# First recurrent mixer of a fused seven-stage network: four modulation units moved to later stages, the border to the next stage in the common form, the last turns gathered behind one output unit

## The chip, the cores and the metric

The kernel runs on one core of one Trainium2 chip. The metric is the time of one execution in microseconds (us), as the device reports it. Before the change three runs gave 1424.58, 1425.66 and 1426.38 us, the median being 1425.66.

Engines in this text: TensorE (PE: products; its weight loads are PEld), VectorE (DVE), ScalarE (ACT), GpSimd (POOL) and SyncE (SP), which issues all transfers from HBM.

## The reference

The input x has 256 tokens of 1024 values. It goes through six sublayers (feed-forward, mLSTM mixer, feed-forward, feed-forward, Mamba-2 mixer, feed-forward) and one hybrid attention layer. Each sublayer has this form:

```python
def swiglu(h, w1, w3, w2):
    return (jax.nn.silu(h @ w1) * (h @ w3)) @ w2

def sublayer(x, fn, g_pre, g_post, shift, scale, gate, weight):
    hmod = rms_norm(x, g_pre) * (1 + scale[:, None, :]) + shift[:, None, :]
    y = rms_norm(fn(hmod), g_post)
    return x + weight * gate[:, None, :] * y
```

`shift`, `scale` and `gate` are the modulation: three vectors of 1024 per sublayer, from a matrix of 1024 x 9216 per layer of three sublayers:

```python
c_act = jax.nn.silu(c)
mod = (c_act @ ada_w[i] + ada_b[i]).reshape(B, N_SUB, 3, D_MODEL)
```

The mLSTM mixer projects to queries, keys, values and an output gate for 4 heads, computes the heads, normalises each, multiplies it by the sigmoid of the gate and ends with the output product `hs.astype(h.dtype) @ w_out`, with `w_out` of 1024 x 1024. All is float32.

## The kernel before, in words

**Stages.** The seven sublayers are stages n = 0 to 6 (`KIND`): ffn, ml, ffn, ffn, mb, ffn, hy. Stage 1 (ml) is the first recurrent mixer, stage 2 the second feed-forward. Each engine has one program that is written out by hand, stage after stage; its instructions run in that order, and semaphores order the engines among each other.

**Weights.** All weights come in units of 1 MB (128 x 2048 float32), numbered through the whole kernel; `FIRST[n]` is a stage's first. A unit is loaded by SyncE into one of five places of a ring (`raw`), rounded by ScalarE (`hi(u)`, L558) and its remainder is computed by VectorE (`lo(u)`, L1704, or in four quarters by `lo_part`, L1709). The remainder is written over the raw unit. TensorE computes each float32 product as three: high x high, high x low, low x high. A place is free when TensorE has used the unit for both halves of the tokens (t = 0 and 1, 128 tokens each); SyncE waits for that before the load. At the borders before stages 1, 3, 4, 5 and 6 the next stage's second unit (`outside`) and its fourth (`landing`) are loaded into two other areas, so that they can come before ring places are free. Stage 2 does not have that.

**Modulation units.** The modulation matrices come in units of 1 MB as well (`load_ada`, into two places `araw` that alternate). VectorE multiplies each with c and sums it up in two products of 128 x 1024 (`ada(v)`, L1714). They serve no product of TensorE; they only have to be done before the stage that they modulate: shift and scale before the stage's input is made (`mod_columns`), the gate before its output is added (`gate_columns`). `ADA_FIRST` and `ADA_BLOCKS` set which are done in which stage. The mixer does ten, 26 to 35: six among its recurrence, one each behind `denominator(3)`, behind `turned_lo(0, ...)` and behind `turned_lo(1, ...)`, and the tenth in the border. Stages 2 and 3 do 18 each, two ahead of block 2 and two per block in blocks 2 to 9.

**End of the mixer.** The last pair of heads is made by VectorE (`heads_out(1)`, L2030) once ScalarE has the sigmoid of the output gate (L752). TensorE turns the heads by 128 x 128 (`turn_am`, L1367), ScalarE copies them out as high parts (`turned_hi`, L790) and VectorE as remainders (`turned_lo`, L2061). The output product has four units, each used for t = 0 and t = 1 (`down`). Units 0 and 1 need the first pair of heads, units 2 and 3 the last.

**Border.** Between two stages: y (the output product) of one half of the tokens is squared by ScalarE (`square_y`, L623) and multiplied by the gate by VectorE (`gated_y`, L1801); GpSimd makes the norm (L474, L475); VectorE makes the new x (`new_x`, L1808); ScalarE squares it (L615); GpSimd makes the second norm; VectorE scales it (`normed_x`, L1770); TensorE turns it (`turn_x`, L1154); ScalarE and VectorE modulate it and split it into high part and remainder (L639, L643, L1779). TensorE hides this for t = 0 behind the output product for t = 1, and for t = 1 behind the first products of the next stage (`first_two`). `boundary(n, late)` is that border on ScalarE and VectorE: the common form has `late` False; the form behind stage 1 has `late` True and takes in the remainders of the next stage's first four weights and a modulation unit.

**Feed-forward.** 11 blocks of two up units and, two blocks behind, one down unit; each block is six groups of twelve products and four turns of 128 x 128 (L1263).

## Time and profile before

| | |
|---|---|
| median of three runs | 1425.66 us (1424.58 to 1426.38) |
| profiled execution: span from the first to the last instruction | 1421.9 us |
| profiled execution's own time around the span | not given on the page |
| mean granted TensorE clock | 0.998 of the full 2.4 GHz |
| busy: PE, PEld, DVE, ACT, POOL | 1394.5, 1185.4, 1024.9, 719.7, 90.4 us |
| moved from HBM | 339.07 MB, 238 GB/s on average |
| stage 1 with its border | about 228 to 345 us |
| stage 2, stage 3 | about 324 to 516 us, 516 to 705 us |

A line of the timeline has its start in us from the span's start, its length in us, the engine, the line of the kernel, the operation with what it writes and reads, how many instructions are merged, and in brackets how long the engine was idle before it and what released it. The ends of products are modelled, since products are pipelined: where one follows at once, the distance of two starts tells the time of one. "L1045" is the helper through which all weight products go, "L1704" is that of all whole remainders, "L558" that of all roundings.

### The profile page before, as it was taken

How to read it: one execution, taken by the hardware profiler on the slowest of the kernel's cores; microseconds unless marked ns; L12 is line 12 of the kernel's file. 1: busy time of each engine (PE TensorE's matmuls, PEld its weight loads, DVE VectorE, ACT ScalarE, POOL GpSimd, SP SyncE). 2: the span in 40 equal slices, each digit the busy share in tenths (PEclk: the TensorE clock that was granted, in tenths of full speed). 3: DMA queues.
4: the chain of work that ended last, by engine and by line, in shares of the span. 5: the costliest groups of instructions: out<-in, count | busy, mean ns of one | idle time of the engine just before them, and what ended most of it. 6: DMA issues, size and time to landing. Idle time of an engine off the chain costs nothing.

```text
span 1421.9 us, 18024 instructions
## 1 busy us (share of the span) xinstructions
PE 1394.5 (98%) x7310; PEld 1185.4 (83%) x7310; DVE 1024.9 (72%) x1296; ACT 719.7 (51%) x931; POOL 90.4 (6%) x118
## 2 busy tenths in 40 slices
PE   9999999998999999999999999999999999999997
PEld 8788888977888878888789978788888889998886
DVE  5887677987987668777767976678745654664865
ACT  5543356456444455343565676554334644555433
POOL 1000001001000010000000352100000100000000
PEclk9999999999999999999999999999999999999999
DMA  9898865855988848888535522478755454445542
GB/s 385 339 351 303 319 247 198 320 193 201 391 308 298 325 162 324 318 311 332 200 135 186 209 74 89 178 299 336 283 206 207 178 204 167 148 170 186 199 149 111
DMA packets 50498, 339.07 MB, mean 238 GB/s; under 512 B 6720, under 2 KB 8432, under 8 KB 10352
## 3 DMA queue, kind: packets, MB, share of 16 engines
q1 hardware_dynamic: 50416, 337.92, 63.8%
q8 instruction: 58, 0.95, 0.3%
q14 instruction: 24, 0.20, 0.0%
HBM read 336.81 MB, written 2.66 MB: 239 GB/s over the span
## 4 chain that ended last, share of the span: by engine, by line
PE 78%; DVE 12%; ACT 4%; DMA 2%; issue 2%; POOL 1%; SPq 0%; ACTq 0%; DVEq 0%; POOLq 0%
PE ps L1045 76%; DVE wlo L1704 4%; DMA raw<-units 2%; DVE hf L2126 2%; DVE M L1714 1%; ACT whi L558 1%; PE ps L1263 1%; PE ps L1154 1%; ACT hf L639 0%; POOL base L474 0%; POOL ssx L475 0%; DVE xboth L1779 0%; DVE wlo L1709 0%; PE ps L1528 0%; DVE xboth L2061 0%
## 5 line engine op out<-in xcount | busy, mean ns | idle before, releaser
L1045 PE MATMUL ps<-whi,xboth 128*128 128x512 f32 x2864 | 912.2, 393 | 6.5 <-DVE wlo L1709 1.7
L1045 PEld LDWEIGHTS ps<-whi,xboth 128*128 128x128 f32 x2864 | 538.3, 188 | 125.4 <-issue 4.7
L1704 DVE TENSOR_TENSOR wlo<-raw,whi 128x2048 fp32r<-128x2048 f32 x212 | 486.2, 2298 | 178.5 <-ACT whi L558 178.0
L1045 PE MATMUL ps<-wlo,xboth 128*128 128x512 f32 x1432 | 558.5, 390 | 0.0
L558 ACT ACTIVATE whi<-raw 128x2048 fp32r<-128x2048 f32 x218 | 416.9, 1915 | 170.8 <-DMA raw<-units 170.7
L1045 PEld LDWEIGHTS ps<-wlo,xboth 128*128 128x128 f32 x1432 | 269.5, 188 | 52.6
L1045 PE MATMUL ps<-xboth,whi 128*128 128x256 f32 (+1 forms) x1152 | 254.6, 310 | 0.1
L1045 PEld LDWEIGHTS ps<-xboth,whi 128*128 128x128 f32 x1152 | 187.9, 190 | 12.4 <-ACT hf L829 0.3
L1045 PE MATMUL ps<-xboth,wlo 128*128 128x256 f32 x704 | 198.1, 281 | 0.0
L1714 DVE SCALAR_TENSOR_TENSOR M<-M 128x1024 f32<-128x1024 f32 x160 | 189.3, 1220 | 0.1
L1045 PEld LDWEIGHTS ps<-xboth,wlo 128*128 128x128 f32 x704 | 133.9, 190 | 0.0
L722 ACT ACTIVATE xboth<-ps 128x512 fp32r<-128x512 f32 x44 | 26.3, 598 | 129.1 <-PE ps L1263 129.1
L718 ACT ACTIVATE M<-ps 128x256 f32<-128x256 f32 x88 | 33.2, 380 | 91.0 <-PE ps L1045 88.5
L474 POOL TENSOR_SCALAR base<-ssx 128x1 f32<-128x1 f32 x28 | 17.6, 629 | 950.5 <-ACT M L623 615.1
L1913 DVE TENSOR_TENSOR M<-M,ps 128x256 f32<-128x256 f32 x88 | 36.0, 417 | 29.4 <-ACT M L718 29.2
L1919 DVE TENSOR_TENSOR xboth<-ps,xboth 128x512 fp32r<-128x512 f32 x44 | 30.3, 689 | 21.8 <-ACT xboth L722 21.7
L2126 DVE SCALAR_TENSOR_TENSOR hf<-hf,cols 128x253 f32<-128x253 f32 (+2 forms) x72 | 36.8, 553 | 7.8 <-ACT hf L829 6.8
L1779 DVE TENSOR_TENSOR xboth<-hf,xboth 128x256 fp32r<-128x256 f32 x42 | 17.9, 446 | 25.0 <-ACT xboth L643 24.6
L639 ACT ACTIVATE hf<-ps,shT,g1T 128x128 f32<-128x128 f32 x60 | 23.8, 446 | 20.5 <-PE ps L1154 20.5
L615 ACT ACTIVATE M<-x 128x512 f32<-128x512 f32 x28 | 17.7, 631 | 26.7 <-DVE x L1808 24.9
L1045 PE MATMUL ps<-unit_at,xboth 128*128 128x512 f32 x120 | 28.9, 389 | 0.0
L1263 PEld LDWEIGHTS ps<-ident,M 128*128 128x128 f32 x176 | 21.7, 140 | 6.8 <-DVE M L1913 0.7
(242 smaller groups left out, 881.2 us busy)
## 6 DMA issues: line engine op xcount, KB each, us to landing
raw<-units SPq DMA_DIRECT2D x218, 1024.0 KB, 4.9
M<-ada_units SPq DMA_DIRECT2D x82, 1024.0 KB, 7.1
M<-units SPq DMA_DIRECT2D x10, 1024.0 KB, 5.3
gp<-gate_rows SPq DMA_DIRECT2D x7, 512.0 KB, 6.1
bias_copies<-bias_by_distance SPq DMA_DIRECT2D x1, 1536.0 KB, 9.6
M<-cvec SPq DMA_DIRECT2D x2, 512.0 KB, 4.4
x<-x_in SPq DMA_DIRECT2D x1, 1024.0 KB, 6.0
ada_a<-ada_units SPq DMA_DIRECT2D x1, 1024.0 KB, 20.0
```

What stands on the lines that cost most here:

```text
L558: act.activation(rounded(u), landed(u), ACT.Copy).then_inc(w_hi, 1)
L639: r = act.activation(hf[:, k, t_], ps[:, 2 * t + q // 2, (k % 4) * P:(k % 4 + 1) * P], ACT.Identity, scale=g1T[:, n, k:k + 1], bias=shT[:, ...
L718: act.activation(sil[:, t, :], ps[:, bank, 0:FB], ACT.Silu).then_inc(sil_ok[t], 1)
L722: act.activation(xhi[:, 8 + 2 * (i % 4):10 + 2 * (i % 4), :], ps[:, 6, :], ACT.Copy)\
L1045: return pe.matmul(out, lhsT, rhs, start=start, stop=stop, skip_group_check=True)
L1263: r = pe.transpose(ps[:, 6, kk * SEQ + t * P:kk * SEQ + (t + 1) * P], g[i % 2][:, t, kk * P:(kk + 1) * P], ident[:, :])
L1704: dve.tensor_tensor(rest(u), landed(u), rounded(u).bitcast(F32), ALU.subtract).then_inc(w_lo, 1)
L1714: return dve.scalar_tensor_tensor(out=w, in0=w, scalar=1.0, in1=cb, op0=ALU.mult, op1=ALU.mult, accum_out=sums[:, column:column + 1])
L1779: dve.tensor_tensor(xlo[:, k2, t_], hf[:, k2, t_], xhi[:, k2, t_].bitcast(F32), ALU.subtract)\
L1913: dve.tensor_tensor(g[i % 2][:, t, :], sil[:, t, :], ps[:, bank, FB:2 * FB], ALU.mult)\
L1919: dve.tensor_tensor(xlo[:, j:j + 2, :], ps[:, 6, :].rearrange("p (a b) -> p a b", b=SEQ), xhi[:, j:j + 2, :].bitcast(F32), ALU.subtract).t ...
L2126: r = dve.scalar_tensor_tensor(out=cacc[:, q, sh:SEQ], in0=cin[:, q, 0:SEQ - sh], scalar=cols[:, col:col + 1], in1=cacc[:, q, sh:SEQ], op0 ...
```

## The change

It does these things:

- Mixer, stage 1: six modulation units (26 to 31) instead of ten. Those behind `denominator(3)`, behind both `turned_lo` and in the border are gone; `ada_done` and `mod_columns` for the next stage stand ahead of `heads_out(1)`.
- Stages 2 and 3 do 20 each, 32 to 51 and 52 to 71: blocks 4 and 6 have three. The gate's columns of stage 2 are made in its block 4.
- Stage 2's second and fourth weight units are loaded outside the ring, as those of the other stages, and the border is the common form, without its `late` branches.
- VectorE: `heads_out(1)` stands ahead of the remainder of the third output unit.
- TensorE: the output product goes (t, unit) = (0,0), (1,0), (0,1), (0,2), (0,3), (1,1), (1,2), (1,3) instead of (0,0), (0,1), (0,2), (0,3), (1,0), ... (1,3). The turns of the last pair stand together behind (0,0) instead of half inside and half behind (0,1).

```diff
-ADA_FIRST = {0: 8, 1: 26, 2: 36, 3: 54, 5: 72}
-ADA_BLOCKS = {0: 9, 2: 9, 3: 9, 5: 6}
+ADA_FIRST = {0: 8, 1: 26, 2: 32, 3: 52, 5: 72}
+ADA_LAST = {0: 25, 1: 31, 2: 51, 3: 71, 5: 83}
+def ada_in_block(n, i):
+    if i > {0: 9, 2: 9, 3: 9, 5: 6}[n]:
+        return 0
+    return 3 if n in (2, 3) and i in (4, 6) else 2
...
-        outside = {FIRST[n] + 1: n for n in (1, 3, 4, 5, 6)}
-        landing = {FIRST[n] + 3: n for n in (1, 3, 4, 5, 6)}
+        outside = {FIRST[n] + 1: n for n in range(1, 7)}
+        landing = {FIRST[n] + 3: n for n in range(1, 7)}
...
-                        sp.wait_ge(a_used[u in outside], (ADA_FIRST[n - 1] + 2 * ADA_BLOCKS[n - 1] - 2 - EARLY) // 2 + 1)
+                        sp.wait_ge(a_used[u in outside], (ADA_LAST[n - 1] - EARLY) // 2 + 1)
...
-                    if n == 3:
+                    if n in (2, 3):
                         sp.wait_ge(w_lo, u0 + 4)
                     load_ada(v)
                     load(down_unit(n, 0))
-                    if n in (3, 5):
+                    if n in (2, 3, 5):
                         sp.wait_ge(w_used, u0 + 2)
                     load_ada(v + 1)
...
-                        for _ in range({6: 1, 7: 1, 8: 0, 9: 0, 10: 2, 15: 2}.get(u, u > 10)):
+                        for _ in range({6: 1, 7: 1, 10: 2, 11: 1, 12: 1}.get(u, 0)):
                             load_ada(v)
...
+                    load(FIRST[n + 1] + 1)
...
# ScalarE, stage 1
-                    hi(u0 + 16)
-                    boundary(n, True)
+                    for u in range(16, 19):
+                        hi(u0 + u)
+                    boundary(n)
...
# TensorE, stage 1
-                    for t in range(T):
-                        for u in range(4):
-                            if t == 0 and u == 2:
-                                turn_am(1, (1,))
-                            pe.wait_ge(S["ml_lo"], 2 * (u // 2) + t + 1)
-                            middle = None
-                            if (t, u) == (0, 1):
-                                middle = lambda: turn_am(1, (0,))
-                            if (t, u) == (1, 3):
-                                middle = lambda: turn_x(n + 1, 0)
-                            r = down(u0 + 12 + u, 2 * u, t, start=(u == 0), stop=(u == 3), middle=middle)
...
+                    for t, u in ((0, 0), (1, 0), (0, 1), (0, 2), (0, 3), (1, 1), (1, 2), (1, 3)):
+                        if (t, u) == (1, 0):
+                            turn_am(1, (0, 1))
+                        pe.wait_ge(S["ml_lo"], 2 * (u // 2) + t + 1)
+                        r = down(u0 + 12 + u, 2 * u, t, start=(u == 0), stop=(u == 3),
+                                 middle=(lambda: turn_x(n + 1, 0)) if (t, u) == (1, 3) else None)
...
# VectorE, border: the late branches are gone
-                if late:
-                    ada(ADA_FIRST[n] + 9)
-                    ada_done(ADA_FIRST[n] + 9)
-                    mod_columns(n + 1)
-                else:
-                    lo_part(u + 2, 1)
-                    lo_part(u + 2, 2)
+                lo_part(u + 2, 1)
+                lo_part(u + 2, 2)
...
# VectorE, feed-forwards
-                            ada(v + 1)
-                            v += 2
-                        if n == 0 and i == 4:
+                        for k in range(1, some):
+                            ada(v + k)
+                        v += some
+                        if n in (0, 2) and i == 4:
                             ada_done(v - 1)
-                            gate_columns(0)
+                            gate_columns(n)
...
# VectorE, stage 1
-                    ada(v + 6)
                     after_piece(5, u0 + 8)
                     turned_lo(0, (0, 1))
-                    ada(v + 7)
+                    ada_done(v + 5)
+                    mod_columns(n + 1)
+                    heads_out(1)
                     after_piece(7, u0 + 8)
-                    heads_out(1)
                     turned_lo(1, (0,))
                     lo(u0 + 15)
                     turned_lo(1, (1,))
-                    ada(v + 8)
-                    boundary(n, True)
+                    lo(u0 + 16)
+                    boundary(n)
```

How this moves instructions, in the order in which they stand. VectorE, end of the mixer, before, from ahead of the last pair of heads to the new x of the first half. The wide products on `M,sums` are modulation units, `wlo` are remainders of weights, `M<-ps 128x256 x4` the last pair of heads, `xboth<-ps,cols,xboth` their turned remainders, `M<-ps,gp` the gated y:

```order
L1714 SCALAR_TENSOR_TENSOR M,sums<-M 128x1024 x2
L1704 TENSOR_TENSOR wlo<-raw,whi 128x2048
L2025 TENSOR_TENSOR M<-M 128x4
L2030 SCALAR_TENSOR_TENSOR M<-ps,M 128x256 x4
L2061 SCALAR_TENSOR_TENSOR xboth<-ps,cols,xboth 128x128 x4
L1704 TENSOR_TENSOR wlo<-raw,whi 128x2048
L2061 SCALAR_TENSOR_TENSOR xboth<-ps,cols,xboth 128x128 x4
L1714 SCALAR_TENSOR_TENSOR M,sums<-M 128x1024 x2
L1801 TENSOR_TENSOR M<-ps,gp 128x512 x2
L1808 SCALAR_TENSOR_TENSOR x<-M,ssx,x 128x512 x2
L1714 SCALAR_TENSOR_TENSOR M,sums<-M 128x1024 x2
L1731 TENSOR_TENSOR shT<-sums,cols 128x8
```

The same place after the change:

```order
L1732 SCALAR_TENSOR_TENSOR g1T<-modc,cols 128x8
L2008 TENSOR_TENSOR M<-M 128x4
L2013 SCALAR_TENSOR_TENSOR M<-ps,M 128x256 x4
L1703 TENSOR_TENSOR wlo<-raw,whi 128x2048
L2044 SCALAR_TENSOR_TENSOR xboth<-ps,cols,xboth 128x128 x4
L1703 TENSOR_TENSOR wlo<-raw,whi 128x2048
L2044 SCALAR_TENSOR_TENSOR xboth<-ps,cols,xboth 128x128 x4
L1703 TENSOR_TENSOR wlo<-raw,whi 128x2048
L1703 TENSOR_TENSOR unit_at_51<-M,unit_at_49 128x2048
L1708 TENSOR_TENSOR wlo<-raw,whi 128x512
L1800 TENSOR_TENSOR M<-ps,gp 128x512 x2
L1807 SCALAR_TENSOR_TENSOR x<-M,ssx,x 128x512 x2
```

Four lines of modulation units are gone (the one at the top here, two further down, and one above the rows shown), the heads stand ahead of the third output unit's remainder, and three remainders of the next stage (`wlo`, `unit_at_51`, and a quarter) stand ahead of the gated y.

TensorE, output product of the mixer, before, around the turns of the last pair (`ident,M`), which stand in two groups of four with half a block between them:

```order
L1045 MATMUL ps<-wlo,xboth 128x512
L1045 MATMUL ps<-whi,xboth 128x512
L1367 MATMUL ps<-ident,M 128x128 x4
L1045 MATMUL ps<-whi,xboth 128x512
L1045 MATMUL ps<-wlo,xboth 128x512
L1045 MATMUL ps<-whi,xboth 128x512 x2
L1045 MATMUL ps<-wlo,xboth 128x512
L1045 MATMUL ps<-whi,xboth 128x512
L1367 MATMUL ps<-ident,M 128x128 x4
L1045 MATMUL ps<-whi,xboth 128x512
```

After, the eight turns stand together behind the first block, with whole blocks on either side:

```order
L1049 MATMUL ps<-whi,xboth 128x512 x2
L1049 MATMUL ps<-wlo,xboth 128x512
L1049 MATMUL ps<-whi,xboth 128x512
L1371 MATMUL ps<-ident,M 128x128 x8
L1049 MATMUL ps<-whi,xboth 128x512
L1049 MATMUL ps<-wlo,xboth 128x512
L1049 MATMUL ps<-whi,xboth 128x512 x2
L1049 MATMUL ps<-wlo,xboth 128x512
L1049 MATMUL ps<-whi,xboth 128x512 x2
```

Each group of `whi`, `wlo`, `whi` is one high x high, high x low, low x high product of 128 x 128 by 128 x 512; a block has twelve.

VectorE, feed-forward of stage 2, around its block 4, before:

```order
L1704 TENSOR_TENSOR wlo<-raw,whi 128x2048
L1714 SCALAR_TENSOR_TENSOR M,sums<-M 128x1024 x2
L1704 TENSOR_TENSOR wlo<-raw,whi 128x2048
L1714 SCALAR_TENSOR_TENSOR M,sums<-M 128x1024 x2
L1919 TENSOR_TENSOR xboth<-ps,xboth 128x512
L1704 TENSOR_TENSOR wlo<-raw,whi 128x2048
L1913 TENSOR_TENSOR M<-M,ps 128x256 x2
```

And after:

```order
L1703 TENSOR_TENSOR wlo<-raw,whi 128x2048
L1713 SCALAR_TENSOR_TENSOR M,sums<-M 128x1024 x4
L1742 TENSOR_TENSOR gpc<-sums,cols 128x8
L1743 SCALAR_TENSOR_TENSOR gpc<-gpc,cols 128x8
L1703 TENSOR_TENSOR wlo<-raw,whi 128x2048
L1713 SCALAR_TENSOR_TENSOR M,sums<-M 128x1024 x2
L1902 TENSOR_TENSOR xboth<-ps,xboth 128x512
L1703 TENSOR_TENSOR wlo<-raw,whi 128x2048
```

The modulation unit at the block's end has become two (x4 products instead of x2), and the gate's columns of stage 2 stand behind them. Block 6, and blocks 4 and 6 of stage 3, have the x4 as well, without the gate's columns.

## Rows read from the trace of the kernel before

**Rows 1.** The page, section 1: busy time, share of the span, instructions.

```profile
PE 1394.5 (98%) x7310; PEld 1185.4 (83%) x7310; DVE 1024.9 (72%) x1296; ACT 719.7 (51%) x931; POOL 90.4 (6%) x118
```

**Rows 2.** TensorE's waits, 296 to 345: line, releaser: total, times, longest.

```profile
PE ps L1045 <- DVE wlo L1709: 1.7, 1, 1.7
PE ps L1045 <- DVE xboth L1779: 1.2, 1, 1.2
...
PE ps L1045 <- DVE wlo L1704: 0.7, 1, 0.7
```

**Rows 3.** Timeline of TensorE, turns of the last pair.

```profile
304.30 0.39 PE L1045 MATMUL ps<-whi,xboth 128*128 128x512 f32 x1
305.39 0.66 PE L1367 MATMUL ps<-ident,M 128*128 128x128 f32 x4 [0.70 <-DVE M L2030]
...
307.28 0.60 PE L1367 MATMUL ps<-ident,M 128*128 128x128 f32 x4
308.44 0.50 PE L1045 MATMUL ps<-whi,xboth 128*128 128x512 f32 x1 [0.56 <-DVE xboth L2061]
```

**Rows 4.** The chain of waits, a steady piece: start, length, what.

```profile
376.95 16.38 PE ps L1045 x72
```

**Rows 5.** Timeline of VectorE, 299 to 315.

```profile
299.77 1.22 DVE L1714 SCALAR_TENSOR_TENSOR M<-M 128x1024 f32<-128x1024 f32 x1
...
302.06 2.29 DVE L1704 TENSOR_TENSOR wlo<-raw,whi 128x2048 fp32r<-128x2048 f32 x1
...
304.46 1.66 DVE L2030 SCALAR_TENSOR_TENSOR M<-ps,M 128x256 f32<-128x256 f32 x4
...
314.21 1.41 DVE L1801 TENSOR_TENSOR M<-ps,gp 128x512 f32<-128x512 f32 x2 [0.31 <-PE ps L1045]
```

**Rows 6.** Timeline of ScalarE, 300 to 323.

```profile
300.65 0.60 ACT L752 ACTIVATE M<-ps 128x512 f32<-128x512 f32 x1 [0.31 <-PE ps L1045]
...
309.51 1.92 ACT L558 ACTIVATE whi<-raw 128x2048 fp32r<-128x2048 f32 x1 [0.46 <-DMA raw<-units]
...
322.11 1.92 ACT L558 ACTIVATE whi<-raw 128x2048 fp32r<-128x2048 f32 x1 [3.07 <-DMA raw<-units]
```

**Rows 7.** Timeline of TensorE, turns of input and of feed-forward, stage 2.

```profile
323.54 1.03 PE L1154 MATMUL ps<-ident,M 128*128 128x128 f32 x8
...
350.92 0.60 PE L1263 MATMUL ps<-ident,M 128*128 128x128 f32 x4
```

**Rows 8.** Timeline of TensorE, the same turns at three common borders.

```profile
515.91 1.09 PE L1154 MATMUL ps<-ident,M 128*128 128x128 f32 x8 [0.30 <-DVE M L1770]
...
538.99 0.60 PE L1263 MATMUL ps<-ident,M 128*128 128x128 f32 x4
...
705.00 1.09 PE L1154 MATMUL ps<-ident,M 128*128 128x128 f32 x8 [0.99 <-DVE M L1770]
...
917.30 1.09 PE L1154 MATMUL ps<-ident,M 128*128 128x128 f32 x8 [0.67 <-DVE M L1770]
```

**Rows 9.** Timeline of all engines, 697 to 699.

```profile
697.25 0.60 ACT L623 ACTIVATE M<-ps 128x512 f32<-128x512 f32 x1 [1.59 <-PE ps L1045]
...
698.37 1.28 DVE L1801 TENSOR_TENSOR M<-ps,gp 128x512 f32<-128x512 f32 x2
```

**Rows 10.** Timeline of SyncE's queue, 302 to 303.

```profile
302.54 0.43 SPq L287 DMA_DIRECT2D raw<-units  x1
```

**Rows 11.** The page, section 6: KB each, median us to landing.

```profile
raw<-units SPq DMA_DIRECT2D x218, 1024.0 KB, 4.9
```

**Rows 12.** Stretches: span, busy us of each engine, clock, DMA, GB/s.

```profile
351.00:371.00 20.00, 20.00 (x94) 16.61 (x93) 19.78 (x23) 11.12 (x10) 0.00 (x0) 1.00 1.02 424
421.50:438.30 16.80, 16.80 (x78) 13.89 (x77) 12.89 (x15) 6.62 (x6) 0.00 (x0) 1.00 0.84 310
574.00:591.00 17.00, 17.00 (x78) 14.07 (x77) 13.06 (x15) 6.90 (x6) 0.00 (x0) 1.00 0.83 310
```

**Rows 13.** Timeline of VectorE, a remainder of block 6, stage 2.

```profile
435.15 2.29 DVE L1704 TENSOR_TENSOR wlo<-raw,whi 128x2048 fp32r<-128x2048 f32 x1 [1.39 <-ACT whi L558]
```

63 lines of the change are left out of this document (23 added, 40 removed).

## Prediction, made before the result was known

> **What bounds the kernel now.** I read the page's busy line first. TensorE is busy for 1394.5 of 1421.9 us [rows 1], so the kernel ends when TensorE has got through its products, and only places where TensorE stands still can give time back. The list of TensorE's waits shows where: between 296 and 345 us, the end of the first recurrent mixer and its border to the second feed-forward, it stood idle for VectorE five times: 1.7, 1.2 and 0.7 us in the first products of the feed-forward [rows 2], behind parts of the weights and of the normalised input that VectorE still had to split, and 0.70 and 0.56 us around the turns of the mixer's last pair of heads [rows 3]. TensorE's timeline gives the losses from start to start, VectorE's and ScalarE's say what those two were doing meanwhile, and the borders of the other stages, which already have the common form, say what that form costs. All times stand against one profiled execution with a span of 1421.9 us. The page gives no time around that span; the median of the three runs, 1425.66, lies 3.8 us above it, and I carry that distance over unchanged.
>
> **The turns of the last pair.** A product takes 16.38 / 72 = 0.2275 us, a block of twelve 2.73 [rows 4]. The product at 304.30 is followed at 305.39, 1.09 us on: 0.86 lost. Four turns start at 307.28 and the product behind them at 308.44, 1.16 us on. Eight turns are busy for 1.03 us and four for 0.66 [rows 3, 7], so four cost 0.4, and 0.76 us are lost. Together 1.6 us; by idle time alone it is 0.70 + 0.56 = 1.26, the lower end. The cause is in VectorE's rows: a modulation unit from 299.77, a weight's remainder from 302.06, and only at 304.46 the four products that make the last pair's heads (L2030, 1.66 us) [rows 5]. They could have begun with ScalarE's last sigmoid out, at 300.65 + 0.60 = 301.25 [rows 6]. After the change the unit is gone and the remainder stands behind the heads, so these are made from 301.3 to 303.2 (0.2 for one small operation, then 1.66). The output phase began eighteen products before 304.53, at 300.4, so its first unit for the first half of the tokens ends at 303.2. The turns stand behind it now and find their input ready. Should the heads be late by x, TensorE waits x; I take 0, with 0.5 as upper end. Behind the turns TensorE has two blocks, 5.5 us, while ScalarE and VectorE copy the turned half out; before it had half a block. The remainder behind the heads is done at 305.4, and its unit, the third, is needed at 303.2 + 0.8 + 2 x 2.73 = 309.5.
>
> **The border.** From the turns of the new input's first half at 323.54 to the first turns of the feed-forward at 350.92 are 27.38 us [rows 7]. The same instructions between the second and the third feed-forward, where the form is the common one, take from 515.91 to 538.99, 23.08 us [rows 8]. The common form is thus worth 4.30 us here. This holds the idle times of [rows 2], 1.7 + 1.2 + 0.7 = 3.6 us, which are the lower end, and the slower starts behind them. What VectorE loses is plain: in the late form one modulation unit lies right ahead of the border and one within it, together with the remainders of all four first weights of the feed-forward. In the changed kernel the units are gone, and two weights and a quarter of the third are done ahead of y.
>
> What comes in their place is a wait ahead of the input's turns. From y's first half to these turns the chain square, norm, new x, norm, scaled x runs beside three blocks with the turns inside the last (2.5 x 2.73 = 6.8 us) in the common form, beside four in the late one. Three like borders show 0.30, 0.99 and 0.67 us of idle there [rows 8]. In the one with 0.99 VectorE began on y at 698.37, 1.1 us after ScalarE's first square of the same y at 697.25 [rows 9]. So the wait is set by how late ScalarE and VectorE come to y, whose half is done at 303.2 + 0.8 + 4 x 2.73 = 314.9 in the new order (VectorE began on it at 314.21 before [rows 5]). VectorE: from the first turned half at 305.3 it has 1.1, 2.2 (a remainder), 1.1, 2.2, 2.2 and 0.7 to do, which gives 314.8. The weight: the third unit of the feed-forward takes the place of the first output unit, which is free when both halves have been through it. That was one block after y's first half, at 316.9, and ScalarE, idle for the transfer until then, rounded what landed from 322.11 on [rows 6]: 5.2 us. Now the second half goes through that unit as the second block, so the place is free at 306.7, the unit lands at 311.9, is rounded by 313.8 and a quarter of it split by 314.6 to 315.0. Both come out just as y does. I take 0.5 us; the ends are 0 and 2.0. The upper one comes from the load issued at 302.54 and rounded from 309.51, 6.9 us [rows 6, 10], though that lay behind two modulation units; the page's median is 4.9 [rows 11].
>
> The Trainium skill would make this dearer: "DMA: Bandwidth & Descriptors", section "Bandwidth", has 6.15 us for a load of 1 MB; by it the new wait would be 0.9 us longer and the time 1421.2. The rows of this trace are shorter, and I go by them.
>
> **What moves into the feed-forwards.** The mixer has six modulation units instead of ten: VectorE is rid of 4 x 2 x 1.22 = 9.8 us [rows 5] there, SyncE of four transfers of 1 MB. The second and third feed-forward get two more each, as a third unit in blocks 4 and 6 (counted from 0), and one of them 0.4 us for the gate's columns. Two products of 1.22 us per unit make 2.4 us more for VectorE in such a block. A block takes TensorE 16.8 us, in which VectorE is busy for 12.9 [rows 12] and TensorE never idle; 3.9 us are free, 2.4 to 2.8 asked for: cost 0. The remainders also have a lead. The piece of 72 at 376.95 starts 5.9 us into block 3 [rows 4], so a block starts at 371.1, and block 7 at 438.3. The remainder made at 435.15 is of that block's last weight, used from 438.3 + 5.9 + 5.5 = 449.7 on, 12 us after it is done, and VectorE had waited 1.39 us for ScalarE before it [rows 13]. On SyncE's queue the third unit stands behind the second, and behind it the next weight's load; VectorE had read its place earlier in the same block, so SyncE need not stand. A sixth transfer makes 372 GB/s of 310. The trace has 424 GB/s at 351 to 371, with TensorE at 20.00 of 20.00 us [rows 12]. In the second feed-forward the first modulation units now wait until VectorE has split the fourth weight and TensorE has been through the second; the third feed-forward does so already and loses nothing (its 23.08 us are the measure above). Cost 0; the upper end is the third rival's price.
>
> The Trainium skill speaks against this: the same page, section "Specifications", has 358 GB/s as what HBM gives one core. By it such a block's six transfers would take 17.6 us, 0.8 more than TensorE's block, 3.0 us over the four, and the time would be 1423.3 if nothing hid it. The 424 GB/s do not bear it out for this core, so it changes no chance.
>
> **Sum.** -1.6 (turns) - 4.3 (border) + 0.5 (new wait) + 0 (feed-forwards) = -5.4 us: a span of 1416.5, a time of 1420.3. By the ends -5.9 at best (1419.8) and -1.3 + 0.5 - 3.6 + 2.0 = -2.4 at worst (1423.3), rivals aside.
>
> **Rivals.**
> - *The new border is late.* The transfer takes 6.9, or VectorE slips, since six jobs follow each other between 305 and 315 with nothing to spare. The wait is 2.0 instead of 0.5, the time 1421.8. For it: both chains end within 0.3 us of y. Against: less traffic, with no modulation unit on the way.
> - *Half of it.* The turns are covered, but the border keeps its waits at other products (the fourth weight, the input's second half), since the mixer hands VectorE over later than a feed-forward does. Only the 1.6 us are won: 1424.1. For it: VectorE has no pause from 305 on. Against: the border at 917.30 follows a mixer too and has a wait of 0.67 only [rows 8].
> - *The feed-forwards become bound by VectorE.* If in all four blocks the 2.4 us fell on the path, that is 9.6 us, the time 1429.9: slower. It decides once a block's added work passes the 3.9 us that VectorE has free and the lead of 12 us is used up. For it: VectorE is busy for 19.78 of 20.00 us at 351 to 371 [rows 12], the opening of the same feed-forward. Against: block 4 starts 17 us later, and in its like of the third feed-forward (574 to 591) VectorE is at 13.06 of 17.00.
>
> **How the numbers follow.** Forecast 0.70 (by itself 1419.3 to 1421.3), late border 0.15, half 0.10, bound feed-forwards 0.05. A measurement of this kernel can tell about 0.2%, 2.9 us, from no change, so faster means below 1422.8: 0.70 + 0.15 = 0.85; same 0.10, the half; slower 0.05. The range takes the forecast and the late border, with some 0.5 us at either side for the spread of the runs (1424.58 to 1426.38): 1418.9 to 1422.6. It leaves out the other two, 0.15.
>
> **What would show it.** Right: no idle of TensorE at the turns of the last pair; 23.1 us from the new input's turns to the feed-forward's first turns; 0 to 1 us of idle ahead of the input's turns; blocks of 16.8 us in both feed-forwards. Wrong: ScalarE waiting for the transfer of the feed-forward's third unit past the end of y's first half; idle of TensorE behind blocks 4 or 6; a stretch from turns to turns that stays above 25 us.

## The result

The changed kernel takes 1418.34 us (median of 5 runs, 1417.32 to 1419.72); the kernel before, run beside it, 1425.97 us (5 runs, 1424.58 to 1427.76). The ratio is 0.9946, with a 95% interval of 0.9933 to 0.9958: faster, by 7.6 us. Forecast were 1420.3 us and a range from 1418.9 to 1422.6. The direction and the mechanism were right; the time lies 0.6 us below the low end of the range.

The profiled execution has a span of 1417.9 us and a time of 1419.72, so 1.8 us lie around a span. The same distance stands in a later profile (1415.8 and 1417.62). The profiled execution of before, with its span of 1421.9, was therefore one of some 1423.7 us, 2 us below its median.

Section 1 of the page after, in the form of [rows 1], shows the same work in a shorter span:

```profile
PE 1394.1 (98%) x7310; PEld 1185.3 (84%) x7310; DVE 1023.6 (72%) x1299; ACT 720.1 (51%) x931; POOL 88.1 (6%) x118
```

TensorE has as many products as before and is busy for as long. What is gone is idle time. The list of TensorE's waits from 296 to 346 us, which had five entries before [rows 2, 3], has none after. TensorE's timeline answers to [rows 3] and [rows 7]. It shows the turns of the first and of the last pair of heads (L1371), the turns of the new input (L1158) and the first turns of the feed-forward (L1267):

```profile
295.07 1.03 PE L1371 MATMUL ps<-ident,M 128*128 128x128 f32 x8
...
303.89 0.39 PE L1049 MATMUL ps<-whi,xboth 128*128 128x512 f32 x1
304.12 1.03 PE L1371 MATMUL ps<-ident,M 128*128 128x128 f32 x8
304.91 0.48 PE L1049 MATMUL ps<-whi,xboth 128*128 128x512 f32 x1
...
322.76 1.09 PE L1158 MATMUL ps<-ident,M 128*128 128x128 f32 x8
...
345.85 0.60 PE L1267 MATMUL ps<-ident,M 128*128 128x128 f32 x4
```

No row has a bracket, so none waited. The eight turns start 0.23 us behind the product ahead of them and the next product 0.79 us behind them. From the first pair's turns to the input's are 27.69 us, 29.42 before (294.12, which is the start of the same turns in the trace of before, to 323.54). From the input's turns to the feed-forward's are 23.09 us, 27.38 before. The whole stretch went from 56.80 to 50.78 us, 6.02 less.

VectorE's timeline of that place, which answers to [rows 5]; the last number of a bracketed pair is what released it:

```profile
302.33 0.16 DVE L2008 TENSOR_TENSOR M<-M 128x4 f32<-128x4 f32 x1 [1.17 <-ACT M L755]
302.52 1.66 DVE L2013 SCALAR_TENSOR_TENSOR M<-ps,M 128x256 f32<-128x256 f32 x4
304.10 2.28 DVE L1703 TENSOR_TENSOR wlo<-raw,whi 128x2048 fp32r<-128x2048 f32 x1
...
314.97 0.69 DVE L1708 TENSOR_TENSOR wlo<-raw,whi 128x512 fp32r<-128x512 f32 x1
316.09 1.41 DVE L1800 TENSOR_TENSOR M<-ps,gp 128x512 f32<-128x512 f32 x2 [0.43 <-PE ps L1049]
```

The heads (L2013) now start as soon as ScalarE has their factor, 1.9 us earlier than before by the clock and 2.9 counted from the first pair's turns, and ahead of the remainder. At the other end VectorE is done with its quarter (L1708) and stands 0.43 us idle until TensorE has y: VectorE is no longer the late one. SyncE's and ScalarE's rows at the same place answer to [rows 6, 10]. SyncE's row is the load into the place that the new second output block frees:

```profile
307.92 0.33 SPq L294 DMA_DIRECT2D raw<-units  x1
```

```profile
312.80 1.93 ACT L566 ACTIVATE whi<-raw 128x2048 fp32r<-128x2048 f32 x1 [2.25 <-DMA raw<-units]
316.09 0.60 ACT L631 ACTIVATE M<-ps 128x512 f32<-128x512 f32 x1 [1.37 <-PE ps L1049]
```

The block whose end frees the place of the feed-forward's third unit ended at 304.91 + 2.73 = 307.6. The load was issued at 307.92, and ScalarE rounded what landed from 312.80: 4.9 us after the issue, 5.2 after the place was free. It was done 1.4 us ahead of y.

In the feed-forwards the block with three units is the place to look. Stretches of the changed kernel over blocks 4 and 6 of the second feed-forward; the columns are those of [rows 12]: length, busy time of TensorE, weight loads, VectorE, ScalarE and GpSimd, granted clock, DMA share, GB/s.

```profile
382.90:399.70 16.80, 16.80 (x77) 13.91 (x76) 12.88 (x15) 6.52 (x6) 0.00 (x0) 1.00 0.85 334
416.50:433.30 16.80, 16.80 (x77) 13.89 (x77) 14.13 (x16) 7.01 (x6) 0.00 (x0) 1.00 0.91 370
```

TensorE is busy for all 16.80 us in both. Its turns start 16.8 us apart in every block of full length, from 371.3 to 489.0 us, and the third unit costs nothing. VectorE works ahead of TensorE: its four products of block 4's last two units stand from 398.69 us on, in the stretch behind the first of these two, where nothing is lost either.

The gain of 6.02 us in the stretch is less than the 7.6 us between the medians. The rest of the span against before's: the start is 0.95 us later (295.07 for 294.12), the way to the turns of the third border 0.75 longer, behind that 0.3. So the two profiled spans differ by only 4.0 us, while the medians differ by 7.6. How far executions scatter was the first thing to settle.

### The profile page after: what moved, and what is told of

The parts are those of the page before. It is cut to its first block, busy times and chain, and to the rows that moved or that the text cites. A ratio compares the mean times of both kernels' runs of the same rounds, so it can differ in the third digit from the quotient of the medians.

```text
span 1417.9 us, 18027 instructions
## 1 busy us (share of the span) xinstructions
PE 1394.1 (98%) x7310; PEld 1185.3 (84%) x7310; DVE 1023.6 (72%) x1299; ACT 720.1 (51%) x931; POOL 88.1 (6%) x118
## 4 chain that ended last, share of the span: by engine, by line
PE 81%; DVE 9%; ACT 4%; DMA 3%; issue 2%; POOL 1%; SPq 0%; ACTq 0%; POOLq 0%; DVEq 0%
PE ps L1049 78%; DMA raw<-units 3%; DVE wlo L1703 3%; DVE hf L2109 2%; ACT whi L566 1%; PE ps L1267 1%; PE ps L1158 1%; DVE M L1713 0%; ACT hf L647 0%; POOL ssx L483 0%; PE ps L1527 0%; POOL base L482 0%; DVE xboth L1778 0%; ACT xboth L651 0%; PE ps L1631 0%
## 5 line engine op out<-in xcount | busy, mean ns | idle before, releaser
L1703 DVE TENSOR_TENSOR wlo<-raw,whi 128x2048 fp32r<-128x2048 f32 x210 | 481.2, 2296 | 178.4 <-ACT whi L566 177.9
L1896 DVE TENSOR_TENSOR M<-M,ps 128x256 f32<-128x256 f32 x88 | 35.6, 416 | 26.5 <-ACT M L721 26.4
L1902 DVE TENSOR_TENSOR xboth<-ps,xboth 128x512 fp32r<-128x512 f32 x44 | 30.2, 687 | 20.0 <-ACT xboth L725 19.9
L1049 PE MATMUL ps<-unit_at,xboth 128*128 128x512 f32 x144 | 34.7, 390 | 0.0
L1049 PEld LDWEIGHTS ps<-unit_at,xboth 128*128 128x128 f32 x144 | 27.0, 188 | 5.7
```

The lines of the kernel that those rows point to most:

```text
L1049: return pe.matmul(out, lhsT, rhs, start=start, stop=stop, skip_group_check=True)
L1703: dve.tensor_tensor(rest(u), landed(u), rounded(u).bitcast(F32), ALU.subtract).then_inc(w_lo, 1)
L1896: dve.tensor_tensor(g[i % 2][:, t, :], sil[:, t, :], ps[:, bank, FB:2 * FB], ALU.mult)\
L1902: dve.tensor_tensor(xlo[:, j:j + 2, :], ps[:, 6, :].rearrange("p (a b) -> p a b", b=SEQ), xhi[:, j:j + 2, :].bitcast(F32), ALU.subtract).t ...
```

## The experiments

Each kernel ran beside the kernel before on the same chip. In the table, "turns" is TensorE's stretch from the first pair's turns to those of the new input, "border" from there to the first turns of the feed-forward; "second mixer" is from the turns of the border ahead of stage 4 to those of the border behind it. These are starts in one profile each.

| kernel | turns | border | sum | second mixer | median us (runs) | before us (runs) | ratio, interval |
|---|---|---|---|---|---|---|---|
| before, first profile | 29.42 | 27.38 | 56.80 | 212.3 | | | |
| after, first profile | 27.69 | 23.09 | 50.78 | 212.4 | 1418.34 (5) | 1425.97 (5) | 0.9946, 0.9933 to 0.9958 |
| before again | 29.42 | 27.38 | 56.80 | 216.3 | 1425.39 (12) | 1425.72 (29) | 0.9999, 0.9986 to 1.0011 |
| after again | 27.69 | 23.07 | 50.76 | 216.4 | 1419.33 (6) | 1425.72 (29) | 0.9953, 0.9939 to 0.9968 |
| turns alone | 28.17 | 27.37 | 55.54 | 213.7 | 1423.48 (12) | 1425.72 (29) | 0.9984, 0.9973 to 0.9995 |
| units alone | 28.55 | 27.35 | 55.90 | 212.4 | 1424.31 (12) | 1425.72 (29) | 0.9990, 0.9976 to 1.0003 |
| place late | 35.14 | 24.39 | 59.53 | 216.5 | 1429.69 (9) | 1425.45 (15) | 1.0023, 1.0009 to 1.0037 |
| columns ahead | 27.68 | 23.06 | 50.74 | 213.7 | 1420.30 (7) | 1425.45 (15) | 0.9964, 0.9951 to 0.9978 |
| four in a block | 27.69 | 23.07 | 50.76 | 216.4 | 1434.28 (6) | 1425.45 (15) | 1.0064, 1.0042 to 1.0085 |
| columns in last block | 27.68 | 23.06 | 50.74 | 212.4 | 1417.24 (6) | 1425.67 (11) | 0.9942, 0.9926 to 0.9958 |
| after once more | 27.68 | 23.09 | 50.77 | 213.7 | 1418.49 (6) | 1425.67 (11) | 0.9956, 0.9940 to 0.9973 |
| order, late form | 27.62 | 28.33 | 55.95 | 212.4 | 1424.14 (12) | 1426.05 (17) | 0.9987, 0.9973 to 1.0001 |

### Both kernels again: is the stretch steady?

The kernel before, nothing edited. Expected:

> The kernel before, unchanged, run against itself. What is open: the change was measured at 7.6 us between medians, while the two profiled executions differ by 4.0 us in span (1421.9 and 1417.9) and by 6.0 us in the stretch from the first pair's turns of the mixer to the first turns of feed-forward 2. Theory A: all that the change does is in that stretch, 5.9 to 6.0 us, and the rest is scatter of single executions in places that it does not touch. Then this gives a ratio of 1.000, and its stretch from the first pair's turns to the feed-forward's first turns is 56.8 us as in the known profile, wherever its own time lies. Theory B: the late form of the border is itself unsteady, and the known profile of before caught it at its shortest. Then this profile's time is near 1426 and that stretch is 1.5 to 2 us longer than 56.8.

The changed kernel, nothing edited. Expected:

> The changed kernel, unchanged, against the one before, for a second measure of the gain. Theory A: 5.9 us plus or minus the scatter, a ratio of 0.9958 with an interval that holds it; its stretch from the first pair's turns to the feed-forward's first turns is 50.8 us again, no idle of TensorE ahead of the turns of the new input behind the mixer, and 0 to 1 us ahead of those of the other borders. Theory B: 7.5 us again, a ratio of 0.9947.

And it once more in a later job, to size what lies beyond the stretch. Expected:

> The changed kernel once more, nothing edited, beside the kernel before on the same chip. My theory is that the change is worth what the stretch from the first pair's turns to the first feed-forward's turns lost, 56.8 to 50.8 us, and that everything beyond is scatter between executions (the clock granted in the second recurrent mixer): the stretch 50.8 again, the gain 5.5 to 6.5 us, a ratio near 0.9956. Rival: the borders and blocks behind it gain too, a steady 1 to 2 us more, as the first measure of 7.6 us has it: a ratio at or below 0.9947, and the time between the turned input of the fourth border and that of the fifth shorter than in the kernel before in every profile.

The stretch is steady: 56.80 and 56.80 us before, 50.78, 50.76 and 50.77 after. So no border of before is seen that is late in some executions only; the two experiments below that keep it whole have 27.37 and 27.35 us too. The spans, though, are 1421.9 and 1428.0 before and 1417.9, 1421.0 and 1418.5 after, and most of that stands in one column of the table, the second recurrent mixer, whose code the change leaves alone. Stretches of it, granted clock in the third column from the right. Before, first and second profile:

```profile
820.00:870.00 50.00, 44.99 (x309) 38.34 (x308) 35.66 (x34) 36.48 (x86) 27.60 (x16) 0.97 0.18 64
```

```profile
820.00:870.00 50.00, 45.94 (x305) 38.99 (x303) 33.50 (x30) 36.24 (x85) 26.76 (x16) 0.93 0.19 67
870.00:925.00 55.00, 53.45 (x253) 45.08 (x252) 32.58 (x45) 29.58 (x45) 5.27 (x8) 0.94 0.42 152
```

After, the second profile:

```profile
820.00:870.00 50.00, 46.43 (x309) 40.43 (x308) 35.23 (x35) 32.61 (x77) 26.61 (x16) 0.91 0.18 64
```

TensorE stands still for some 3.6 to 5 of 50 us there, and the granted clock of these stretches lies between 0.91 and 0.97. The executions with 0.93 and 0.91 take 216.3 and 216.4 us for the mixer, the two with 0.97 take 212.3 and 212.4. Over the whole mixer, turns to turns, all twelve profiles of this text fall in line: a mean granted clock of 0.99 in the five that take 212.3 to 212.4 us, 0.98 in the three with 213.7, 0.97 in the four with 216.3 to 216.5. So both kernels scatter by about 4 us for a reason that has nothing to do with the change, and one execution of each can't size it.

The three measures of the change are 7.6, 6.4 and 7.2 us. Over all runs the changed kernel has a median of 1419.1 us (17 runs) and the kernel before 1425.7 (89 runs): 6.6 us. The 6.02 us of the stretch are a ratio of 0.9958, which is the upper end of the first interval and within the two others. The ratio of 0.9947 or less that the rival asked for did not come back. A part of what lies above 6.02 us is the mix of clocks: among executions with a mean granted clock of 0.998, the median is 1425.16 us before (40 runs) and 1419.12 after (8), 6.0 us apart, and with 0.999 it is 1423.76 (12) and 1417.47 (3), 6.3 apart. At 0.995 or below are 25 of the 89 runs of before and only 2 of the 17 of after. All five runs of the first measure of the changed kernel had 0.998 or 0.999.

### The turns alone

Before, with only the turns' part of the change:

```diff
-                            if t == 0 and u == 2:
-                                turn_am(1, (1,))
+                            if (t, u) == (0, 1):
+                                turn_am(1, (0, 1))
-                            if (t, u) == (0, 1):
-                                middle = lambda: turn_am(1, (0,))
...
-                    after_piece(7, u0 + 8)
                     heads_out(1)
+                    after_piece(7, u0 + 8)
```

> The kernel before with only the turns of the last pair changed: the eight turns stand together behind output block (0,0), and the last pair of heads stands ahead of the third output unit's remainder on VectorE. All ten modulation units and the late border stay, and the other output blocks keep their order. My theory: the heads are made from 302.1 to 304.0 in the time of before (a modulation unit ends at 302.06), the first turns find them, the second four wait 0.4 us: of the 1.6 us lost there 1.2 are won, and the border, with all its waits, stays: ratio 0.9992. Rival: what is won at the turns is lost again in the border, since VectorE is what is late there and has as much to do: ratio 1.000, the idle times of the border longer by 1.2 in sum.

The turns took 1.25 us less and the border as long as before (27.37). The waits of TensorE's products between 296 and 352 us are what the border had before, [rows 2], and none at the turns; its weight loads (the last line) still waited 0.6 us there for the heads:

```profile
PE ps L1045 <- DVE wlo L1707: 1.7, 1, 1.7
PE ps L1045 <- DVE xboth L1777: 1.2, 1, 1.2
PE ps L1045 <- DVE wlo L1702: 0.7, 1, 0.7
PEld ps L1367 <- DVE M L2028: 0.6, 2, 0.4
```

The turns and the border are two losses with two causes, as the prediction had it. The time, 2.2 us less, has 1.25 within its interval.

### The modulation units alone

Before, with the tables and loops of the modulation units as after, but the late border, the old order of the output product and of the heads:

```diff
-ADA_FIRST = {0: 8, 1: 26, 2: 36, 3: 54, 5: 72}
+ADA_FIRST = {0: 8, 1: 26, 2: 32, 3: 52, 5: 72}
...
-                    ada(v + 6)
-                    ada(v + 7)
-                    ada(v + 8)
...
-                    ada(ADA_FIRST[n] + 9)
-                    ada_done(ADA_FIRST[n] + 9)
+                    ada_done(ADA_FIRST[n] + 5)
```

> The kernel before with only the modulation units moved (six in the mixer, 20 each in feed-forwards 2 and 3, the gate's columns in block 4); the order of the output product and the late border, with its weights in the ring, stay. My theory: VectorE's work is not what the border waits for alone. The first of the two losses at the turns goes (0.86), the second (0.76) stays; in the border the scaled x comes no earlier, since it waits for GpSimd's norm, and the remainders still follow it: 0.3 us. Together 1.2 us, ratio 0.9992. Rival: the four modulation units are the cost, 9.8 us of VectorE's time, and most of the gain comes with them alone: 4 us or more, ratio 0.997.

```profile
PE ps L1052 <- DVE wlo L1716: 1.7, 1, 1.7
PE ps L1052 <- DVE xboth L1786: 1.2, 1, 1.2
PE ps L1052 <- DVE wlo L1711: 0.6, 1, 0.6
PE ps L1052 <- DVE xboth L2066: 0.6, 1, 0.6
```

Expected were 1.2 us, measured 0.90. Of the five waits one is gone, that for the heads. The border's three stand as they were, although two modulation units have left VectorE there. So it wasn't the units' own 9.8 us that held TensorE in the border. The interval of the times reaches above 1, so it is the stretch that tells this, not the median.

### The order without the common form

That kernel, with the new order of the output product, the eight turns together, and the heads ahead of the remainder, but still the late border:

```diff
-                    for t in range(T):
-                        for u in range(4):
...
+                    for t, u in ((0, 0), (1, 0), (0, 1), (0, 2), (0, 3), (1, 1), (1, 2), (1, 3)):
+                        if (t, u) == (1, 0):
+                            turn_am(1, (0, 1))
...
-                    after_piece(7, u0 + 8)
                     heads_out(1)
+                    after_piece(7, u0 + 8)
```

> The kernel before with the modulation units moved, the output product in the new order with the eight turns together behind its first block, and the heads of the last pair ahead of the third output unit's remainder; but the border of this mixer keeps its late form (the remainders of the feed-forward's four first weights made within the border, its second and fourth unit loaded in the ring). My theory: order and units give the 1.6 to 2.2 us around the last pair's turns and nothing in the border, whose remainders are made as late as before and still hold TensorE for 1.2, 0.6 and 1.7 us: from the first pair's turns to the feed-forward's 54.6 to 55.0 us (56.8 before, 50.8 with the whole change), the time 2 us less, a ratio near 0.9985. So the form is worth the remaining 4 us, and only together with the order (the common form with the old order gave 59.5). Rival: the order alone gives most of it, since the new second block frees the ring's place three blocks sooner, the fourth weight is there earlier and its remainder no longer late: 51 to 52.5 us, a ratio of 0.996 to 0.997.

The sum is 55.95 us, no better than with the units alone and 1 us above what I expected. The turns take 27.62 us, all of their gain, and the border 28.33, almost a microsecond more than before. TensorE's waits, 296 to 356:

```profile
PE ps L1052 <- DVE wlo L1711: 1.7, 1, 1.7
PE ps L1052 <- DVE wlo L1706: 1.0, 1, 1.0
PE ps L1052 <- DVE xboth L1781: 1.0, 1, 1.0
PE ps L1052 <- DVE xboth L1786: 0.4, 1, 0.4
```

VectorE sets the end of this border. It scales the new x from 321.78 on, 27.08 us behind the first pair's turns, as before (321.40, 27.28 behind): y's first half comes to it 21.02 us behind them instead of 20.09, since the new order puts one more block ahead of it. From there it works through the late remainders almost without a pause, and the last wait for one of them ends at 338.33, which is 43.6 us behind the first pair's turns; 44.5 before. TensorE came earlier and waited longer. Both theories missed, mine by the 1 us and the rival by 4. What the form is worth on top of units and order is thus 55.95 - 50.77 = 5.2 us.

### The common form with the old order

The changed kernel with the output halves one after the other. The place of the feed-forward's third weight comes free later:

```diff
-                    for t, u in ((0, 0), (1, 0), (0, 1), (0, 2), (0, 3), (1, 1), (1, 2), (1, 3)):
-                        if (t, u) == (1, 0):
+                    for t, u in ((0, 0), (0, 1), (0, 2), (0, 3), (1, 0), (1, 1), (1, 2), (1, 3)):
+                        if (t, u) == (0, 1):
```

> The changed kernel with the output product in its old order by halves, (0,0), turns, (0,1), (0,2), (0,3), (1,0), ... (1,3): only output block (1,0) is moved back behind y's first half. My theory: the order is what lets the common border stand, since the first output unit's place takes the feed-forward's third unit. It is free 2.7 us after y's first half instead of 8.2 before it; the load takes 5.1, the rounding 1.9, a quarter's remainder 0.7, and ScalarE's square and VectorE's product of y stand behind them. The chain of 7.1 us starts 10.5 us after y's half, the turns of the new input come 8 us late: the stretch from the first pair's turns to the feed-forward's first turns is 58.7 us instead of 50.8, ratio 1.0013. Rival: the place of the load does not matter, the order only moved the turns: 50.8 us, ratio 0.9958.

SyncE, ScalarE, VectorE and TensorE in turn:

```profile
315.12 0.33 SPq L294 DMA_DIRECT2D raw<-units  x1
```

```profile
320.04 1.92 ACT L566 ACTIVATE whi<-raw 128x2048 fp32r<-128x2048 f32 x1 [10.47 <-DMA raw<-units]
```

```profile
321.99 0.69 DVE L1708 TENSOR_TENSOR wlo<-raw,whi 128x512 fp32r<-128x512 f32 x1 [7.91 <-ACT whi L566]
322.60 1.28 DVE L1800 TENSOR_TENSOR M<-ps,gp 128x512 f32<-128x512 f32 x2
```

```profile
329.25 1.12 PE L1158 MATMUL ps<-ident,M 128*128 128x128 f32 x4 [7.36 <-DVE M L1769]
```

The load is issued when the place is free, lands 4.9 us later, and behind it hang the rounding, the first quarter and only then y. TensorE stands 7.4 us, and the sum is 59.53 (58.7 expected). The second output block for the other half of the tokens is what makes the common form possible: it has the place free three blocks, 8.2 us, earlier (12.6 us behind the first pair's turns for 20.8). This measures the new wait of the prediction from its other side. With the place 8.2 us late it is 7.4 us, with the place as it is now it is nothing.

### Four units in a block

The changed kernel with blocks 4 and 6 of both feed-forwards at four units instead of three, and one block fewer with any:

```diff
-    if i > {0: 9, 2: 9, 3: 9, 5: 6}[n]:
+    if i > {0: 9, 2: 8, 3: 8, 5: 6}[n]:
...
-    return 3 if n in (2, 3) and i in (4, 6) else 2
+    return 4 if n in (2, 3) and i in (4, 6) else 2
```

> The changed kernel with four modulation units in blocks 4 and 6 of feed-forwards 2 and 3 instead of three, and none in their block 9 (20 each as before): it doubles what the change added there. VectorE's added work in such a block is 4.8 us, over the 3.9 that it has free, and SyncE waits with the fourth until VectorE has read the second, 5 to 6 us, with the next weight's load behind it. My theory: the lead of 12 us over TensorE covers both, no idle of TensorE, 151.8 us between the first and the last turns of each feed-forward as before, ratio 0.9958. Rival, the one of a bound VectorE: what passes the free time falls on the path, 1 us or more per block, 4 us or more in all, ratio 0.9986 or above, and the 151.8 us grow by 2 us or more.

I had expected the lead of 12 us to cover it. It did not. Two blocks of each feed-forward take some 19 and 21 to 22 us instead of 16.8, 13.7 us in all, and the kernel is slower than before. Here is where it goes, in the order of time (SyncE twice, ScalarE, VectorE and TensorE). The first row is the fourth unit, the second the weight's load behind it:

```profile
400.10 0.33 SPq L305 DMA_DIRECT2D M<-ada_units  x1
400.47 0.43 SPq L294 DMA_DIRECT2D raw<-units  x1
...
407.71 1.92 ACT L566 ACTIVATE whi<-raw 128x2048 fp32r<-128x2048 f32 x1 [12.25 <-DMA raw<-units]
...
416.96 0.74 DVE L1896 TENSOR_TENSOR M<-M,ps 128x256 f32<-128x256 f32 x2
...
417.43 0.50 PE L1049 MATMUL ps<-whi,xboth 128*128 128x512 f32 x1 [1.94 <-DVE M L1896]
```

The same load and rounding in the changed kernel, with three units, where the first pair's turns lie 0.98 us later:

```profile
394.26 0.33 SPq L294 DMA_DIRECT2D raw<-units  x1
...
401.04 1.92 ACT L566 ACTIVATE whi<-raw 128x2048 fp32r<-128x2048 f32 x1 [4.58 <-DMA raw<-units]
```

SyncE must wait with a fourth unit until VectorE has read its place, and the next weights stand behind it in SyncE's queue: their load is issued at 400.47 instead of 394.26. ScalarE waited 12.25 us for a weight, 4.58 with three units, and VectorE's next remainder began at 409.66 instead of 403.75. What TensorE then misses is not the remainder with its long lead but the gated product (L1896), which VectorE makes behind those remainders and units and which frees TensorE's banks. So the price of the prediction's third rival is real, with its edge between three and four units, but its mechanism is not the one seen. VectorE's added work passes its 3.9 us by 0.9 us in such a block, 3.6 us over the four, and the loss is 13.7. VectorE itself stood idle for 2.85 us before the fourth unit (waiting for the transfer) and 1.59 us before that remainder (waiting for ScalarE). What came late is the weight, behind the fourth unit in SyncE's queue, and the short lead decides, that of the gated product. No run has the four units with their loads in another order, so the share of VectorE's own work is not split off.

### The columns behind the last feed-forward block

The borders behind the first three feed-forwards keep a wait ahead of the input's turns, in both kernels. Small VectorE operations stand there, the columns of scale, shift and gate. The changed kernel with these ahead of the last remainder of the gated values:

```diff
-                    gated_lo(NF - 1)
                     ada_done(v - 1)
                     for k in {0: (1,), 2: (3,), 3: (4, 5), 5: (6,)}[n]:
                         mod_columns(k)
                         gate_columns(k)
+                    gated_lo(NF - 1)
```

> The changed kernel with the small column operations of the modulation (shift, scale, gate: 0.7 us per stage, 1.5 in stage 3) ahead of the last remainder of the gated values in each feed-forward instead of behind it, where VectorE waits anyway. My theory: the idle of TensorE ahead of the input's turns (0.25, 0.56 and 0.99 us behind stages 0, 2 and 3) comes from VectorE reaching y 0.6 to 1.1 us late, and these operations are ahead of it there: all three go, 1.5 us or a little more from start to start, ratio 0.9947 against the kernel before (0.9958 for the change). Rival: VectorE is held by ScalarE's rounding of the next weights, which is not earlier, and the operations move for nothing: 0.9958, the three idle times as they were.

TensorE's waits from 490 to 715 us, in the changed kernel and then in this one:

```profile
PE ps L1158 <- DVE M L1769: 1.5, 2, 1.0
```

```profile
PE ps L1049 <- DVE xboth L1902: 2.5, 2, 1.7
PE ps L1158 <- DVE M L1769: 0.2, 1, 0.2
```

The wait moved to the remainder (L1902) and grew. My theory fell. Then the same operations one block earlier, where VectorE has slack:

```diff
                         gated_lo(i - 1)
+                        if i == NF - 1:
+                            ada_done(v - 1)
+                            for k in {0: (1,), 2: (3,), 3: (4, 5), 5: (6,)}[n]:
+                                mod_columns(k)
+                                gate_columns(k)
```

> The changed kernel with the small VectorE operations that form the columns of scale, shift and gate (and those of the gates) taken from behind the remainder of the last gated values into the last feed-forward block, right behind the remainder before it and ahead of the last two products; the remainder of the last gated values then runs at once behind its products. My theory: TensorE's waits of 0.25, 0.56 and 0.99 us before the turned input at the borders behind the first three feed-forwards go, and no product of the last output units waits longer, since the operations now stand in slack of the block: those three borders, from the last block's turns to the turned input, take about 12.8 to 13.3 us in place of 13.54, 13.91 and 14.30, the time is 1.8 to 3.3 us below the changed kernel's, near 1416 to 1418, a ratio near 0.993 to the kernel before. Rival: the last products' values come later by the 2 to 4 small operations, some 0.5 to 1.5 us, and TensorE waits for the rounded or the remaining part of them instead: borders of 13.5 to 14.5, a ratio of 0.995 to 0.996.

```profile
PE ps L1049 <- DVE xboth L1902: 0.5, 1, 0.5
PE ps L1158 <- DVE M L1769: 0.2, 1, 0.2
```

The three borders take 12.78, 13.98 and 13.13 us, in the changed kernel on the same chip 12.78, 14.56 and 14.42: 1.9 us less in the profile. Two of the three came as forecast; behind the second feed-forward, waits of 0.24 us before the turns and 0.5 us for the remainder (L1902) stayed. The medians are 1417.24 and 1418.49. It is the fastest kernel measured here, but its interval overlaps that of the changed kernel, so only the profile shows that it beats it.

## Why the prediction came out as it did

**The turns of the last pair: right.** Forecast -1.6 us. The stretch up to the input's turns lost 1.73. By itself the part gave 1.25. That this equals the idle time of [rows 3] is chance: with a modulation unit still ahead of them the heads' products began at 302.99, 8.1 us behind the first pair's turns instead of 7.4, the weight loads of the eight turns waited for them, and the turns took 1.20 us from start to start instead of 0.79. In the changed kernel the heads began at 302.33. The prediction's 301.3 is 302.25 on the clock of this trace, in which the first pair's turns lie 0.95 us later, so they came as worked out, and the turns did not wait.

**The border: right.** Forecast -4.3 us from the comparison with the next border; measured 27.38 - 23.09 = 4.29. Reading the price of a form from its twin in the same trace was better than the sum of the waits, which would have given 3.6.

**The reason given for it: partly wrong.** The text put the loss down to modulation units and late remainders. The units alone left all three waits, so what is left is the rest of the form: where the remainders stand, and the loads outside the ring. TensorE's waits name the remainders, and together the two are worth 5.2 us; no run splits them. The form in turn needs the new order (59.53 us without it), and the order gives nothing in the border without the form (55.95). The parts don't add up one by one: -0.9, -1.3 and +2.7 alone or nearly alone, -6.0 together.

**The new wait: the step that failed.** The text had "I take 0.5 us; the ends are 0 and 2.0". Measured was 0, the lower end, in all three profiles. The two chains ahead of y came out within 0.3 us of what was worked out (VectorE done at 315.66, the load in 5.2 us), and y came at 316.09, just behind them. The text gives no working for the 0.5 us; its own two chains end as y does, which is no wait. The value stands beside the 0.30, 0.99 and 0.67 us of the like borders of [rows 8], and seems to be carried over from them. In the two of these that lie behind a feed-forward, the small operations for the columns stand ahead of y, and the experiments with them showed that they make most of the wait. This mixer makes its columns before the heads, at 300.7 to 301.2 us. What makes the 0.67 us of the border behind the second mixer was not tried. The Trainium skill, "DMA: Bandwidth & Descriptors", section "Bandwidth", has 6.15 us for 1 MB in a table of transfers issued from GpSimd; here SyncE issues them. With it in place of the 5.2 us, the quarter would have been done at about 316.4, and VectorE some 0.3 us late to y (an estimate from that figure and the rows above). The rows have 4.9 us from the issue here and in the kernel with the place late.

**The feed-forwards: right, at three units.** Cost 0, with blocks of 16.8 us at 370 GB/s. By the 358 GB/s in "Specifications" of the same page, block 6 would have been late. It was not; the traffic there is above that figure.

**The range: too narrow at the low end.** With the new wait at 0 and the turns at 1.73 the sum is -6.0 us and the time 1425.66 - 6.0 = 1419.6, inside the range. So the mis-sized term alone does not carry the time out of it; the rest of the distance, 1419.6 to 1418.34, is of the size by which medians of five or six runs differ. The two other medians were 1419.33, inside, and 1418.49. The range had allowed some 0.5 us for the spread of the runs, from three runs of before with 1.8 us between them. With 29 runs beside each other on one chip it is 1421.7 to 1429.6, and the three medians of the changed kernel differ by 1.0 us.

**What lay around the span: read wrongly, without effect.** The text called the 3.8 us between span and median the time around the span. It is 1.8; the other 2 were that this execution was a short one. As the sum was made of differences, it did not enter.

**What stays open.** Between 6.0 us in the stretch and 6.6 over all runs (7.6, 6.4 and 7.2 by job) lie 0.6 us. No stretch outside shows a steady gain in three profiles of after and two of before, none of the intervals rules out 6.0, and at equal granted clock the medians are 6.0 and 6.3 us apart. Most of the 0.6 is thus likely the mix of clocks; whether anything else stands there was not settled.

## What to carry to other kernels

Where a stage has a twin in the same trace in a better form, take the price from the twin, start to start, and ask of every wait carried over from the twin which instructions make it and whether they stand here too. Before costing a freed engine as a gain, find the transfer whose place comes free last: the form paid only because the order of the products freed that place 8.2 us earlier. Size the range by the scatter of many runs. For a unit added to a block, look at what its transfer waits for and what is queued behind it, and then at the shortest lead, not the longest.

## What the runs showed of the hardware

- In an unchanged mixer, in the middle of which TensorE stands for 3.6 to 5 of 50 us, the mean granted clock lay between 0.97 and 0.99 from one execution to the next, and the mixer took between 212.3 and 216.5 us, the longer the lower the clock.
- A load of 1 MB issued at 315.12 us was rounded from 320.04 on, 4.9 us. Behind a fourth modulation unit that had to wait for its place, ScalarE waited 12.25 us for its weight.
- One core moved 370 GB/s over a block in which TensorE never stood, and 424 over the opening of the same feed-forward [rows 12].
